# Triangular inverse in a gated DeltaNet layer: the 16-row diagonal blocks solved by rows on GpSimd from blocks passed through DRAM, with the head's units in the order k, q, v

## The reference, cut to what matters

```python
def gated_delta_rule(q, k, v, g, beta):
    ...
    a_mat = jnp.where(strict, jnp.einsum('bhnid,bhnjd->bhnij', k_beta, k) * decay, 0.0)
    eye = jnp.eye(CHUNK, dtype=jnp.float32)
    t_inv = lax.linalg.triangular_solve(a_mat + eye, jnp.broadcast_to(eye, a_mat.shape),
                                        left_side=True, lower=True, unit_diagonal=True)
    u = jnp.einsum('bhnij,bhnjd->bhnid', t_inv, v * beta[..., None])
    w = jnp.einsum('bhnij,bhnjd->bhnid', t_inv, k_beta * jnp.exp(g)[..., None])
```

## Time and profile before

| | us |
|---|---|
| median of 3 runs | 2252.11 |
| lowest and highest of them | 2247.33, 2254.2 |
| the profiled execution's own time | 2254.17 |
| its span, first to last instruction | 2252.4 |
| PE busy in the span | 2203.3 |
| DVE, ACT, POOL busy | 1121.4, 859.0, 243.3 |

### The profile page before, as it was taken

One profiled execution on the slowest core, in us unless ns is written; L12 is line 12 of the kernel. 1 busy time (PEld: TensorE's weight loads), 2 busy tenths in 40 slices (PEclk: granted clock), 3 DMA queues, 4 the chain that ended last, 5 costly groups with the idle time before them and its releaser, 6 DMA issues.

```text
span 2252.4 us, 26792 instructions
## 1 busy us (share of the span) xinstructions
PE 2203.3 (98%) x10238; PEld 1770.2 (79%) x10238; DVE 1121.4 (50%) x1596; ACT 859.0 (38%) x1102; POOL 243.3 (11%) x163
## 2 busy tenths in 40 slices
PE   7999999999999999999999999899999999999998
PEld 6888887666677888888888888678888877888886
DVE  4444444687644444423444432486676544444423
ACT  4333323224544333322333322557667554333221
POOL 1000000122211000000000000033333201000001
PEclk9999999999999999999999999999999999999999
DMA  5333322212113333332333332211111123333321
GB/s 168 96 93 102 113 91 71 73 57 66 47 57 94 94 102 93 111 100 79 93 93 97 113 103 80 67 38 38 38 38 38 38 76 93 98 98 93 118 94 50
DMA packets 49759, 185.89 MB, mean 83 GB/s; under 512 B 6544, under 2 KB 6544, under 8 KB 49680
## 3 DMA queue, kind: packets, MB, share of 16 engines
q1 hardware_dynamic: 49392, 184.77, 26.8%
q10 hardware_dynamic: 288, 0.03, 0.0%
HBM read 182.68 MB, written 2.10 MB: 82 GB/s over the span
## 4 chain that ended last, share of the span: by engine, by line
PE 91%; DVE 5%; ACT 2%; issue 1%; POOL 0%; DMA 0%; SPq 0%; DVEq 0%; ACTq 0%; POOLq 0%
PE prod L396 27%; PE prod L398 26%; PE prod L397 26%; PE misc L598 4%; PE misc L529 1%; PE prod L486 1%; PE misc L547 1%; DVE qc L1338 1%; PE misc L649 1%; ACT w_hi L736 1%; PE misc L621 1%; DVE w_lo L972 1%; DVE qc L1336 0%; PE misc L509 0%; PE misc L538 0%
## 5 line engine op out<-in xcount | busy, mean ns | idle before, releaser
L972 DVE TENSOR_TENSOR w_lo<-raw,w_hi 128x1024 fp32r<-128x1024 f32 (+1 forms) x300 | 404.8, 1349 | 762.2 <-ACT w_hi L736 761.4
L396 PE MATMUL prod<-h_hi,w_hi 128*128 128x512 f32 x1856 | 764.7, 412 | 0.6 <-DVE w_lo L972 0.3
L398 PE MATMUL prod<-h_hi,w_lo 128*128 128x512 f32 x1856 | 725.8, 391 | 0.0
L397 PE MATMUL prod<-h_lo,w_hi 128*128 128x512 f32 x1856 | 724.8, 391 | 0.0
L736 ACT ACTIVATE w_hi<-raw 128x1024 fp32r<-128x1024 f32 (+1 forms) x317 | 356.0, 1123 | 598.5 <-PE prod L398 586.9
L396 PEld LDWEIGHTS prod<-h_hi,w_hi 128*128 128x128 f32 x1856 | 350.2, 189 | 104.5 <-issue 38.5
L397 PEld LDWEIGHTS prod<-h_lo,w_hi 128*128 128x128 f32 x1856 | 350.2, 189 | 73.5 <-issue 10.6
L398 PEld LDWEIGHTS prod<-h_hi,w_lo 128*128 128x128 f32 x1856 | 349.2, 188 | 74.7
L396 PE MATMUL prod<-a_hi,w_hi 128*128 128x512 f32 x704 | 277.4, 394 | 0.0
L398 PE MATMUL prod<-a_hi,w_lo 128*128 128x512 f32 x704 | 276.0, 392 | 0.0
L397 PE MATMUL prod<-a_lo,w_hi 128*128 128x512 f32 x704 | 273.2, 388 | 0.0
(11 more groups left out here) (226 smaller groups left out, 2070.2 us busy)
## 6 DMA issues: line engine op xcount, KB each, us to landing
raw<-in_w SPq DMA_DIRECT2D x253, 512.0 KB, 3.6
raw<-in_wd SPq DMA_DIRECT2D x64, 704.0 KB, 4.1
x<-in_x SPq DMA_DIRECT2D x8, 256.0 KB, 6.2
out<-y_out SPq DMA_DIRECT2D x8, 256.0 KB, 2.2
consts<-in_consts SPq DMA_DIRECT2D x1, 896.0 KB, 8.6
raw<-in_w SPq DMA_DIRECT2D x2, 256.0 KB, 4.5
hf<-in_pos SPq DMA_DIRECT2D x1, 256.0 KB, 9.7
od_conv<-in_od_conv SPq DMA_DIRECT2D x1, 48.0 KB, 2.2
```

The source lines that it names most:

```text
L396: pe.matmul(bank, wh, hi, start=first and k == 0, stop=False)
L397: pe.matmul(bank, wh, lo, start=False, stop=False)
L398: ins = pe.matmul(bank, wl, hi, start=False, stop=last and k == tiles_n - 1)
L972: dve.tensor_tensor(w_lo[:, n % 2, 0:w], raw[:, n % 4, 0:w], w_hi[:, n % 2, 0:w].bitcast(F32), ALU.subtract).then_inc(lo_ready, 1)
```

## The change

Levels 1 to 4 of the doubling are replaced. The 16x16 diagonal blocks of A (8 per chunk, 32 per head) are written by SP from `a_mat` to a DRAM buffer (8 DMAs, in pieces of 64 bytes), and read back (8 DMAs), so that every one of the 16 partitions of a block holds the whole block, `blk`. POOL then solves the rows of each block's inverse: 15 steps of a multiply and a subtract of at most 4 x 15 elements per partition, each waiting for the one before it. One more operation spreads the rows into `t_inv`. Step `turn` transposes it on PE into `u_inv`. Levels 5 to 7 are as before.

For that, k k^T becomes a step of its own (`kk`, slot -4) ahead of the other products (`gram`, slot 5), units come in the order k, q, v, k is squared and scaled first, and several waits follow. SP's new DMAs stand between two weight loads. The constants have `block` and `block_eye` in place of four masks. The core of the diff, in the order of the file (the tables, SP's loads of this layer, steps of PE, the list of POOL per head):

```diff
-OD_UNITS = [("ba", 0)] + [(w, h) for h in range(HEADS) for w in "qkv"] + [("z", h) for h in range(HEADS)]
+OD_UNITS = [("ba", 0)] + [(w, h) for h in range(HEADS) for w in "kqv"] + [("z", h) for h in range(HEADS)]
...
-CHAIN1 = {"spread": -17, "decay": -13, "mask": -11, "squareq": -12, "normq": -9, "scaleq": -6,
-          "squarek": -4, "normk": -3, "scalek": 0, "gram": 4, "turn1": 7}
-CHAIN1.update({"y2": 11, "t2": 13, "y3": 15, "t3": 17, "y4": 18, "t4": 20, "y5": 21, "t5": 22, "y6": 24, "t6": 25,
-               "y7": 26, "t7": 27})
+CHAIN1 = {"spread": -17, "decay": -13, "mask": -11, "squarek": -12, "normk": -9, "scalek": -6, "kk": -4,
+          "squareq": -4, "normq": -1, "scaleq": 2, "gram": 5, "turn": 12,
+          "y5": 14, "t5": 16, "y6": 18, "t6": 20, "y7": 22, "t7": 24}
...
                 load(OD_N + u, A["w8"][OD0 + u])
+                g = u // 3 - 3
+                if u % 3 == 0 and 0 <= g < HEADS:
+                    sp.wait_ge(a_made, g + 1)
+                    for b in range(BLOCKS):
+                        p = slice(b * BLK, (b + 1) * BLK)
+                        sp.dma_start(blocks[g, b].rearrange("t k j -> k t j"), a_mat[p, :, p]).then_inc(blk_out, 16)
+                    sp.wait_ge(blk_out, 16 * BLOCKS * (g + 1))
+                    if g:
+                        sp.wait_ge(t_made, g)
+                    for b in range(BLOCKS):
+                        sp.dma_start(blk[b * BLK:(b + 1) * BLK].rearrange("p t k j -> p (t k j)"),
+                                     blocks[g, b:b + 1].rearrange("a t k j -> a (t k j)")
+                                     .broadcast_to([BLK, TT * BLK * BLK])).then_inc(blk_in, 16)
...
+                elif name == "kk":
+                    pe.wait_ge(qk_ready, 2 * g + 1)
+                    each(M[0], kn, kn).then_inc(kk_mm, 1)
                 elif name == "gram":
...
-                    each(M[0], kn, kn).then_inc(kk_mm, 1)
...
-                elif name == "turn1":
-                    pe.wait_ge(b_made, LEVELS * g + 1)
-                    pe.wait_ge(a_made, 5 * g + 1)
+                elif name == "turn":
+                    pe.wait_ge(t_made, g + 1)
+                    pe.wait_ge(gram_used, 4 * (g + 1))
                     for t in range(TT):
-                        ins = pe.transpose(M[0][:, t, :], b_lvl[:, 1, t, :], const["ident"])
-                    ins.then_inc(b1_turned, 1)
+                        ins = pe.transpose(M[1][:, t, :], t_inv[:, t, :], const["ident"])
+                    ins.then_inc(t_turned, 1)
...
+                pool.wait_ge(a_made, g + 1)
+                if g:
+                    pool.wait_ge(y_mm, UP * g)
+                for l in (LOW + 2, LOW + 1):
+                    mask(l)
+                pool.tensor_copy(rows[:], const["block_eye"][:, 0:BLK].unsqueeze(1).broadcast_to([P, TT, BLK]))\
+                    .then_inc(rows_seq, 1)
                 pool.wait_ge(qk_ready, 2 * g + 2)
...
+                pool.wait_ge(blk_in, 16 * BLOCKS * (g + 1))
+                seq = (2 * BLK - 1) * g + 1
+                for k in range(BLK - 1, 0, -1):
+                    pool.wait_ge(rows_seq, seq)
+                    pool.tensor_tensor(rows_tmp[:, :, 0:k], blk[:, :, k, 0:k],
+                                       rows[:, :, k:k + 1].broadcast_to([P, TT, k]), ALU.mult).then_inc(rows_seq, 1)
+                    pool.wait_ge(rows_seq, seq + 1)
+                    pool.tensor_tensor(rows[:, :, 0:k], rows[:, :, 0:k], rows_tmp[:, :, 0:k], ALU.subtract)\
+                        .then_inc(rows_seq, 1)
+                    seq += 2
+                pool.wait_ge(rows_seq, seq)
+                if g:
+                    pool.wait_ge(tu_ready, TU * g)
+                pool.tensor_tensor(t_inv[:].rearrange("p t (b j) -> p t b j", j=BLK),
+                                   rows[:].unsqueeze(2).broadcast_to([P, TT, BLOCKS, BLK]),
+                                   same(const["block"]).rearrange("p t (b j) -> p t b j", j=BLK), ALU.mult)\
+                    .then_inc(t_made, 1)
+                pool.wait_ge(t_made, g + 1)
+                pool.wait_ge(y_mm, UP * g + 1)
+                mask(LEVELS)
```

More of the change, by code:

```diff
@@ L60 @@
 ROWS8 = GU3 + 2 * FT
-CONSTS = ["ident", "ones", "tri", "neg_future", "rot", "dup", "dup_rot"] + [f"level{l}" for l in range(1, LEVELS + 1)]
+BLK = 16
+BLOCKS = P // BLK
+LOW = 4
+UPPER = range(LOW + 1, LEVELS + 1)
+CONSTS = ["ident", "ones", "tri", "neg_future", "rot", "dup", "dup_rot", "block", "block_eye"] + [f"level{l}" for l in UPPER]
 def unit_width(n):
@@ L118 @@
 FIRST = 4
+BLK_TILE = 3
 def delta_slots():
@@ L143 @@
 STORES = [(0, "v", 1), (1, "v", 2), (2, "p", 1), (3, "v", 3), (4, "v", 4), (6, "v", 5), (5, "p", 2), (7, "v", 6)]
-TU = 2 * LEVELS - 1
-TM = 2 * (LEVELS - 1) - 1
+UP = LEVELS - LOW
+TU = 2 * UP
+TM = 2 * UP - 1
 N_SIDE = 17
@@ L251, in program @@
         t_inv = od("t_inv", [TT, P])
+        rows, rows_tmp = od("rows", [TT, BLK]), od("rows_tmp", [TT, BLK])
         y_lvl = od("y_lvl", [TT, P])
@@ L272, in program @@
         misc = nc.alloc_psum_tensor("misc", [P, 4, T], F32)
+        blocks = nc.dram_tensor("blocks", (HEADS, BLOCKS, TT, BLK, BLK), F32).ap()
         def tiles(ap):
@@ L303, in program @@
         dec_ready, kk_mm, gram_mm, a_made = sem("dec_ready"), sem("kk_mm"), sem("gram_mm"), sem("a_made")
-        b_made, b1_turned, tu_ready = sem("b_made"), sem("b1_turned"), sem("tu_ready")
+        gram_used, blk_out, blk_in = sem("gram_used"), sem("blk_out"), sem("blk_in")
+        rows_seq, t_made = sem("rows_seq"), sem("t_made")
+        b_made, t_turned, tu_ready = sem("b_made"), sem("t_turned"), sem("tu_ready")
         y_mm, y_ready, t_mm = sem("y_mm"), sem("y_ready"), sem("t_mm")
@@ L604, in stage_pe @@
             def stage_pe(g, name):
-                L = g * (LEVELS - 1)
                 i = g % 2
@@ L608, in stage_pe @@
                     if g >= 1:
-                        pe.wait_ge(tu_ready, TU * (g - 1) + 2)
+                        pe.wait_ge(qk_rstd, 2 * g)
                     pe.wait_ge(gb_ready, g + 1)
@@ L614, in stage_pe @@
                 elif name in ("normq", "normk"):
-                    j = "qk".index(name[-1])
+                    j = "kq".index(name[-1])
                     pe.wait_ge(qk_sq, 2 * g + j + 1)
@@ L652, in stage_pe @@
                     l = int(name[1:])
[L653 to L656, removed]
+                    pe.wait_ge(y_ready, UP * g + l - LOW)
+                    pe.wait_ge(tu_ready, TU * g + 2 * (l - LOW) - 1)
                     each(M[2], t_inv, y_lvl, lambda m: half_blocks(m, l, 1)).then_inc(t_mm, 1)
@@ L894, in stage_act @@
             def stage_act(g, name):
-                L = g * (LEVELS - 1)
                 i = g % 2
                 if name in ("squareq", "squarek"):
-                    j = "qk".index(name[-1])
+                    j = "kq".index(name[-1])
                     act.wait_ge(act_done, 3 * g + j + 1)
-                    act.activation(sq[:, j, :], (qc, kc)[j][:, i, :], ACT.Square).then_inc(qk_sq, 1)
+                    act.activation(sq[:, j, :], (kc, qc)[j][:, i, :], ACT.Square).then_inc(qk_sq, 1)
                 elif name in ("normq", "normk"):
-                    j = "qk".index(name[-1])
+                    j = "kq".index(name[-1])
                     act.wait_ge(qk_sum, 2 * g + j + 1)
@@ L909, in stage_act @@
                         act.wait_ge(qdec_ready, g)
+                        act.wait_ge(gram_used, 4 * g)
                     act.activation(e_row[:], M[0], ACT.Exp).then_inc(e_row_ready, 1)
@@ L943, in _ @@
                         act.wait_ge(gated, h + 1)
+                        if h == BLK_TILE:
+                            act.wait_ge(t_made, HEADS)
                         act.activation(omix_hi[:, h, :], act_f[:, 0, :], ACT.Copy).then_inc(ohi, 1)
@@ L1260, in stage_dve @@
-                    dve.tensor_tensor(kn[:].rearrange("p t c -> p (t c)"), kc[:, i, :], silu_g[:, 1, :], ALU.mult)\
+                    dve.wait_ge(qk_rstd, 2 * g + 1)
+                    dve.tensor_tensor(kn[:].rearrange("p t c -> p (t c)"), kc[:, i, :], silu_g[:, 0, :], ALU.mult)\
                         .then_inc(qk_ready, 1)
+                elif name == "kk":
+                    dve.wait_ge(kk_mm, g + 1)
+                    dve.wait_ge(dec_ready, 2 * g + 1)
+                    if g:
+                        dve.wait_ge(b_made, UP * g)
+                    dve.tensor_tensor(a_mat[:], M[0], dec_a[:], ALU.mult).then_inc(a_made, 1)
@@ L1262, in stage_dve @@
                 elif name == "gram":
                     dve.tensor_copy(e_last[:, i], e_row[:, :, P - 1:P])
-                    dve.wait_ge(kk_mm, g + 1)
-                    dve.wait_ge(dec_ready, 2 * g + 1)
-                    dve.tensor_tensor(a_mat[:], M[0], dec_a[:], ALU.mult).then_inc(a_made, 1)
                     dve.wait_ge(gram_mm, g + 1)
[L1268 to L1274, removed]
```

(29 more changed lines are left out.)

21 lines of the change are left out of this document (10 added, 11 removed).

## The result

The changed kernel takes 2260.99 us (median of 6 runs, 2259.29 to 2263.78), the kernel before 2250.05 in the runs beside it. The ratio is 1.0046, 95% interval 1.0034 to 1.0059: slower, as forecast, but by 10.9 us (0.5%) where 34 (1.5%) was forecast. The profiled execution has a span of 2258.3 us.

A forecast was written before the change was run, and what follows sets the result against it. PE bounds the kernel. Removed steps -52.6, `v_new` waits -8.2, `turn` waits 8 x 9.2 + 9.5, clock tails 12: +34.3 us on 2254.17 gives 2288.5, median 2.1 lower, 2286 us; own range 2266 to 2310, wider 2236 to 2326.

The forecast's parts named there:

- POOL's price: POOL's row solve per head: 30 dependent small operations at 0.25 us fixed each plus 2.1 us, 9.6 us in sum.
- the wait at `turn`: PE waits at slot 12 for POOL's `t_inv`, released at 31.2 us against 22.0 of PE work: 9.2 us per head.
- SP's start: SP's load ahead of the block stores, held up by `w_lo` and POOL's masks, starts 4.6 us after `kk` starts.
- DMA: SP's load, eight stores and eight reads, issued every 0.475 us, landing after 2.2; last read landed at 16.2 us.
- POOL and DVE shutting each other out: From slot 5, DVE's 5.1 us in 8 operations exclude POOL's solve, adding 4.0 us per head.
- What PE has to do until `turn`: PE's own work from the start of `kk` to `turn` in a head: 22.0 us.
- The first two heads: At `turn`, missing older steps lengthen PE's wait by 6.0 us in the first head and 2.6 in the second.
- The tail: After each wait at `turn` PE runs at a lower clock, losing 1.5 us; eight times, 12.
- The removed steps: PE's `y` and `t` steps of the replaced levels: net 6.6 us gone per head, 52.6 over eight.
- That the effects nearly cancel: Rival: `turn` released at 26 to 27 us, 2252 us, within 0.3% of no change; chance 0.08.
- POOL's costlier steps: Rival: POOL's 30 operations take 15 us instead of 9.6, wait grows by 5.4, 2329 us; chance 0.16.
- that DVE takes over: Rival: if the chain fits, DVE adds 1 to 2 us per head, 2243 us; 0.16 together with the chain nearly fitting.

## Why the prediction had the mechanism right and the size wrong

**The mechanism held.** What bounds the kernel, what is removed, where the time goes instead (PE at `turn`, behind SP - DMA - POOL), the end of the `v_new` waits, the unit order at nothing, and POOL's price: 9.6 us for the 30 operations without DVE; the least spacing of each of the thirty over the eight heads sums to 9.9. The fixed part of 0.25 us per dependent operation, taken from three rows of large operations, met 0.29 at 4 elements. The fixed cost of 0.06 us that I had estimated from the Trainium skill (GPSIMD Engine Reference, section "Performance versus the Vector engine") does not hold here: by it operations of 4 elements would follow each other after some 0.14 us, an estimate, and they do after 0.29. The 2257 us that came of it lie nearer to the measured time by luck.

**What failed is the size of one term: the wait at `turn`,** forecast as 8 x 9.2 + 9.5 = 83 us and measured as 63.0. Its parts, per head:
- *SP's start.* Forecast 4.6, measured 3.85 (the load at 1583.77; 3.6 and 4.4 in the first two heads). I had `w_lo` held up by POOL's masks. They did not start at `a_mat`, since they also wait for the previous head's `y7`; they came after `w_lo` (POOL's mask at 1584.12).
- *DMA,* from the load to the first row operation: forecast 11.6, measured 11.7 in this head, 10.7 to 11.7 in all. The parts were off both ways: the reads could start 1.5 us after the last store's issue, not 2.2, and the last reads landed after 3.4 and not 2.2. The microsecond more per direction that stood in the upper bound for pieces of 64 bytes did not show in the stores.
- *POOL and DVE shutting each other out.* Forecast 9.6 + 4.0, measured 12.5, so 2.6 for the exclusion. I charged each of DVE's operations all but 0.15 us. A `w_lo` of 1.2 us did cost POOL 1.0, but a tap only 0.3 to 0.4 and the short ones 0.1. Why POOL's small operations lose less than DVE's time is not shown.
- *What PE has to do until `turn`.* Forecast 22.0, measured 21.5.
- Together the release comes at 28.1 to 29.4 and not 31.2, and a usual wait is 6.9 to 7.9 us and not 9.2: 12 us over the last six heads.
- *The first two heads.* Forecast 15.2 and 11.8, measured 9.7 and 9.1, 8 us less. In the first head PE reached `turn` 19.1 us after `kk`, not 16: short waits (0.8 and 0.6 us) lie in that stretch, and it begins at the lower clock, since `kk` itself waited 3.6 us. PE's timeline at its two ends:

```profile
1452.38 1.16 PE L622 MATMUL misc<-kn 128*128 128x128 f32 x8 [3.60 <-DVE kn L1283]
1453.29 0.56 PE L420 MATMUL prod<-h_hi,w_hi 128*128 128x512 f32 x1
1453.65 0.63 PE L421 MATMUL prod<-h_lo,w_hi 128*128 128x512 f32 x1
...
1471.11 0.40 PE L422 MATMUL prod<-h_hi,w_lo 128*128 128x512 f32 x1
1481.21 1.11 PE L663 MATMUL misc<-consts,t_inv 128*128 128x128 f32 x4 [9.71 <-POOL t_inv L1454]
```

**Two more terms were too small, and nearly cancel.** *The tail* at the lower clock was forecast at 1.5 us per wait, 12 in all. In the head shown it was 2.4: 44.39 us from `kk` to `kk` (1579.92 to 1624.31), less the wait of 7.88, less 34.15. By windows of 0.5 us, the shortfall of the granted clock times PE's busy time sums to 18.2 us behind the eight waits, 1.4 to 3.1 each. *The removed steps* were forecast at 6.6 us per head, 52.6 in all; the forecast had 35.1 us for a head without a wait, and it took 34.15. Before, a head took 43.06 (1587.98 to 1631.04), 41.6 without the wait as listed, so 7.5 us per head are gone, 60 in all. Of the 0.9 too little, 0.3 is the `v_new` wait, listed with 1.4 us: the next matmul started 1.6 late and took 0.1 more. The rest is not taken apart.

What else I left out: PE's other waits over 1450 to 1810, most of them in the first head (for `sq`, `kn` and `vc`), fell from 7.9 to 5.0 us. And one of the six `v_new` waits of before had a tail of 1.7 us; behind the other five the granted clock stayed at 1.00.

```profile
PE misc L612 <- DVE kn L1247: 2.2, 2, 1.8
...
1690.00:1700.00 10.00, 10.00 (x55) 8.38 (x54) 6.27 (x12) 7.71 (x9) 1.27 (x1) 0.83 0.19 52
```

With the measured sizes the sum is -59.8 - 8.2 - 2.9 + 63.0 + 18.2 - 1.7 = +8.6. Measured are +10.9 between the medians and +5.9 between the two profiled spans, so nothing of size stays open; but that the errors of tail and removed steps are about as large as each other is luck. That the removed work is worth some 60 us is shown from the other side too: with the wait gone, the kernel is 46.6 us faster than before, with 5.9 us still waited at `turn` and some 16 us of DVE's lateness, an estimate from 2.2 to 3.3 us in each of six heads, in the place of the 8.2 and 2.9. That gives 57.

**The rivals.** None came true as it stands. That the effects nearly cancel (`turn` released at 26 to 27) came nearest in time, but not by its numbers: the release was at 28.1 to 29.4. POOL's costlier steps are excluded by 9.9 us; that DVE takes over is visible once the wait is gone: with half the row steps a head took 35.8 us, of which 0.6 are the wait at `turn`, 1 us more than 34.15, as that rival had it; with `turn` at 17 it took 3.3 more, above its 1 to 2.

## What to carry to other kernels

When work moves off the bounding engine into a chain of other engines that it waits for in order, the sum of removed instructions says nothing yet: add up the chain from its release, add up what the bounding engine has to do until it asks, and compare. Here the one was 28 to 29 us and the other 21.5, and the same change was worth +11 us with the question asked at slot 12 and -44 at slot 17. For a serial chain of tiny operations count them, not their elements; and place each DMA of such a chain ahead of whatever in its queue waits for somebody else.

## What was not expected of the hardware

- A POOL operation of 4 elements per partition that waits for the one before costs 0.29 us from start to start, one of 60 elements 0.37 to 0.40.
- A `w_lo` of 1.2 us on DVE held up a POOL operation by 1.0, but a POOL operation of 0.3 us is delayed by a tap of 0.75 us on DVE by only 0.3 to 0.4.
- 6.9 us of useless matmuls ahead of each wait made the kernel 14.9 us faster, since PE's clock stayed at 2.4 GHz behind six of the eight.
- A wait costs more than a list of waits shows: 1.44 us listed were 1.61 from start to start, and 0.28 were 0.44.
